# Third tile's stored pairs weighted and added by GpSimd in place of two diagonals on TensorE, in a two-layer retention and expert trunk

## The reference, cut to what matters

```
for l in range(2):
    h = modulate(rmsnorm(x, norm1_g[l]), sh1, sc1)
    x = x + g1 * mixer(h, ...)                 # retention and pooling branches
    h = modulate(rmsnorm(x, norm2_g[l]), sh2, sc2)
    x = x + g2 * moe(h, ...)                   # 16 experts, two for each token
return rmsnorm(x, final_g)

moe: expert_idx, weights = route(h)            # two experts of one group of four
     y[token] = sum over j in (0, 1) of weights[token, j] * expert(expert_idx[token, j], h[token])
```

## Time and profile before

| | |
|---|---|
| median of three runs | 1477.68 us (1476.87 to 1478.13) |
| the profiled execution, its own time | 1476.83 us |
| its span, first to last instruction | 1475.2 us |
| TensorE busy | 1441.6 us (98%) |
| VectorE busy | 1133.5 us (77%) |
| ScalarE busy | 773.2 us (52%) |
| GpSimd busy | 147.6 us (10%) |
| mean granted clock of TensorE | 0.999 of full |

### The profile page before, as it was taken

One profiled execution on the slowest core, in us unless ns is written; L12 is line 12 of the kernel. 1 busy time (PEld: TensorE's weight loads), 2 busy tenths in 40 slices (PEclk: granted clock), 3 DMA queues, 4 the chain that ended last, 5 costly groups with the idle time before them and its releaser, 6 DMA issues.

```text
span 1475.2 us, 18824 instructions
## 1 busy us (share of the span) xinstructions
PE 1441.6 (98%) x6829; PEld 1154.6 (78%) x6829; DVE 1133.5 (77%) x1532; ACT 773.2 (52%) x1102; POOL 147.6 (10%) x139
## 2 busy tenths in 40 slices
PE   7999999999999999999989999999999999999997
PEld 2788877778877778888858888878888787888884
DVE  5774686555669999999977557854345899999998
ACT  4333433222346888888733344242233488888883
POOL 0000001000002211111100000100000122211110
PEclk9999999999999999999999999999999999999999
DMA  9855556455557999999956543642244879999995
GB/s 352 310 185 189 171 199 208 143 177 172 186 213 256 388 387 388 385 387 381 352 221 204 193 132 115 201 142 88 84 171 152 290 279 391 398 387 392 381 379 206
DMA packets 107413, 377.49 MB, mean 256 GB/s; under 512 B 16521, under 2 KB 16713, under 8 KB 106548
## 3 DMA queue, kind: packets, MB, share of 16 engines
q1 hardware_dynamic: 90864, 331.39, 61.6%
q0 software_dynamic: 15200, 40.62, 7.7%
q10 hardware_dynamic: 1252, 4.22, 0.8%
HBM read 361.32 MB, written 34.64 MB: 268 GB/s over the span
## 4 chain that ended last, share of the span: by engine, by line
PE 83%; DVE 12%; DMA 2%; ACT 1%; issue 1%; DVEq 1%; SPq 0%; ACTq 0%
PE ps L1758 25%; PE ps L1760 25%; PE ps L1759 24%; DVE w_lo L1509 3%; DVE w_lo_more L1509 3%; DMA raw<-w 2%; PE ps L1843 2%; PE ps L2017 1%; PE ps L1912 1%; PE ps L2066 1%; PE ps L1916 1%; DVE xgT_lo L1498 1%; DVE y_out L1532 1%; DVE w_lo L1006 1%; PE ps L1947 0%
## 5 line engine op out<-in xcount | busy, mean ns | idle before, releaser
L1006 DVE TENSOR_TENSOR w_lo<-raw,w_hi 128x1024 fp32r<-128x1024 f32 x132 | 161.4, 1224 | 213.2 <-ACT w_hi L650 211.9
L650 ACT ACTIVATE w_hi<-raw 128x1024 fp32r<-128x1024 f32 x132 | 139.1, 1058 | 333.5 <-PE ps L1760 332.5
L1509 DVE TENSOR_TENSOR w_lo<-raw,w_hi 128x1024 fp32r<-128x1024 f32 x188 | 224.6, 1221 | 3.8 <-ACT w_hi L835 3.0
L1758 PE MATMUL ps<-w_hi,hT_lo 128*128 128x512 f32 x512 | 206.2, 403 | 3.8 <-DVE hT_lo L1109 3.1
L1509 DVE TENSOR_TENSOR w_lo_more<-raw,w_hi_more 128x1024 fp32r<-128x1024 f32 x172 | 205.6, 1221 | 2.1 <-ACT w_hi_more L835 1.1
L835 ACT ACTIVATE w_hi<-raw 128x1024 fp32r<-128x1024 f32 x188 | 193.3, 1057 | 22.0 <-DMA raw<-w 12.7
L1760 PE MATMUL ps<-w_hi,hT_hi 128*128 128x512 f32 x512 | 200.0, 391 | 0.0
L1759 PE MATMUL ps<-w_lo,hT_hi 128*128 128x512 f32 x512 | 199.6, 390 | 0.0
L835 ACT ACTIVATE w_hi_more<-raw 128x1024 fp32r<-128x1024 f32 x172 | 176.7, 1057 | 25.2 <-DMA raw<-w 17.1
L1758 PE MATMUL ps<-hT_hi,w_lo 128*128 128x512 f32 x320 | 130.5, 408 | 0.0
L1760 PE MATMUL ps<-hT_hi,w_hi 128*128 128x512 f32 x320 | 124.9, 390 | 0.0
(11 more groups left out here) (285 smaller groups left out, 2632.7 us busy)
## 6 DMA issues: line engine op xcount, KB each, us to landing
raw<-w SPq DMA_DIRECT2D x590, 512.0 KB
h_rows<-h POOLq DMA_DIRECT2D x8, 1024.0 KB, 5.2
ahead<-w SPq DMA_DIRECT2D x4, 2048.0 KB, 11.8
x_state<-x POOLq DMA_DIRECT2D x2, 2048.0 KB, 9.9
y_rows<-x_in ACTq DMA_DIRECT2D x4, 1024.0 KB, 12.0
x<-x_state POOLq DMA_DIRECT2D x4, 1024.0 KB, 7.7
pair_early<-y_rows SPq DMA_DIRECT2D x4, 1024.0 KB, 6.3
x<-x_in SPq DMA_DIRECT2D x4, 512.0 KB, 14.1
```

Of the source, the lines that this page charges most:

```text
L650: act.activation(w_hi[:, q % W_SLOTS], stream_piece(l, q, r), ACT.Copy).then_inc(w_hi_ready, 1)
L1006: v.tensor_tensor(w_lo[:, q % W_SLOTS], stream_piece(l, q, r), w_hi[:, q % W_SLOTS], ALU.subtract).then_inc(raw_used, 1)
L1509: v.tensor_tensor(ring_lo(e * EXP + n), expert_piece(e, n), ring_hi(e * EXP + n), ALU.subtract).then_inc(raw_used, 1)
L1758: pe.matmul(dst, a_lo, b_hi, start=start, stop=False)
```

## The change

VectorE no longer writes `diag_w`, and TensorE no longer runs the four matmuls of f32 on it in each layer. GpSimd gets four instructions in each layer in their place, behind its work for expert 15: it multiplies `pair_2[:, 0]` by its column of weights in place, adds the product to x[:, 2], and does the same with `pair_2[:, 1]`. It waits for `hot_last_ready` and for the load of `pair_2` first, and raises `pairs_added` at the end. VectorE's `last_add` of tile 2 waits for `pairs_added`. Between the layers, `last_rows(l - 1, 2)` now stands before `norm_transposes(l, 0)` on TensorE.

```diff
-                for j in range(2):
-                    one = v.tensor_scalar(diag_w[:, j], ident, w_early[:, 4 * j + 2:4 * j + 3], None, ALU.mult)
                 one.then_inc(hot_last_ready, 1)
@@ last_add
                 v.wait_ge(last_added, l * NT + (t + 1))
+                if t == 2:
+                    v.wait_ge(pairs_added, l + 1)
@@ last_rows (TensorE)
-                                    start=t != 2, stop=True)
+                                    start=True, stop=True)
-            def last_rows_pairs(l):
-                pe.wait_ge(pair_in[2], (l + 1) * PAIR_DMAS[2])
-                pair_matmuls(0)
-                pair_matmuls(1)
@@ TensorE, start of layer 1
-                    last_rows_pairs(l - 1)
+                    last_rows(l - 1, 2)
                     norm_transposes(l, 0)
-                    last_rows(l - 1, 2)
@@ TensorE, end of layer 1
-                    last_rows_pairs(l)
                     last_rows(l, 2)
@@ GpSimd, behind the loop over the experts, in each layer
                     expert(l, e)
+                pool.wait_ge(hot_last_ready, l + 1)
+                pool.wait_ge(pair_in[2], (l + 1) * PAIR_DMAS[2])
+                for j in range(2):
+                    pool.tensor_scalar(pair_2[:, j], pair_2[:, j], w_early[:, 4 * j + 2:4 * j + 3], None, ALU.mult)
+                    pool.drain()
+                    one = pool.tensor_tensor(x[:, 2], x[:, 2], pair_2[:, j], ALU.add)
+                    if j == 0:
+                        pool.drain()
+                one.then_inc(pairs_added, 1)
                 with pool.If(count > 0):
```

More of the change, by code:

```diff
@@ L279, in build @@
         h_nat = sb("h_nat", [P, 2, D], F32, Dr)
-        diag_w = sb("diag_w", [P, 2, P], F32, Dr + 8192)
         h2 = [sb(f"h2_{t}", [P, D], F32, o) for t, o in enumerate((Dr, Dr + 4096, A, A + 4096))]
@@ L419, in build @@
         x_final = sem("x_final")
+        pairs_added = sem("pairs_added")
         ada_mac = sem("ada_mac")
```

## The result

The changed kernel takes 1496.39 us (median of four runs, 1494.40 to 1499.08), the kernel before 1477.91 us in the same comparison (four runs, 1476.87 to 1478.61). The ratio is 1.0128, with a 95% interval of 1.0116 to 1.0140: slower by 18.9 us (17.1 to 20.7). The profiled execution took 1496.41 us, its span is 1494.8 us, 19.6 us more than before. Forecast were 1488.2 us, and 1496 us as the end of the range.

A forecast was written before the change was run, and what follows sets the result against it. The prediction took VectorE to bound the kernel after layer 1 and to be what TensorE waits for between the layers. 6.9 + 1.3 + 2.3 = 10.5 us on 1476.83 us, plus 0.85 us for a median, gave 1488.2 us; range 1482 to 1496 us.

The forecast's parts named there:

- the stop on VectorE: After layer 1: VectorE's first normed output waits for final_g, queued behind GpSimd's arithmetic; 6.9 us, passed whole to the end.
- contention in the tail: After layer 1: GpSimd and VectorE block each other on SBUF, delaying GpSimd and the load; 1.3 us, bounds 0 to 2.6.
- contention between the layers: Between the layers: the two engines on SBUF delay VectorE's hT_lo and so TensorE; 2.3 us, bounds 0 to 4.7.
- So the removed work buys nothing: Both stages: TensorE's diagonals and VectorE's writing of diag_w lie under cover; worth 0, at most 3.4 us at each place.
- worth 0: Between the layers: the diagonals fill the hole before the turned tile 0, so removing them gains 0 us.
- the rival of full exclusion: Tail and between layers: engines exclude each other in full, and TensorE's clock may fall; 16.2 us, 1493.9 us, chance 0.25.
- several us once: On GpSimd: a first elementwise use might cost several us once, hidden in layer 0 up to 753.71; not in the sum.
- never waited at: After layer 1: VectorE's last_add of tile 2 would not wait for GpSimd, being behind the 6.9 us stop.
- the late row: After layer 1: final_g's load into scale_row lands at 1468.5, while VectorE wants it at 1461.62; 6.9 us.
- The middle of the bounds: Tail and between layers: SBUF contention taken midway between none and whole-instruction blocking; 1.3 us and 2.3 us.
- the forecast's own case: Tail and between layers: late row plus middling contention; 10.5 us, 1488.2 us, chance 0.50.
- The other side: Tail: cheap late row, GpSimd at VectorE's 1.22 us, landing 2.6 us, no contention; 2.7 us, 1480.4 us, chance 0.04.

The follow-up runs named there:

- kernel with the row early: Changed kernel with the load of final_g issued ahead of GpSimd's four instructions of layer 1; 1488.34 us, ratio 1.0062.
- kernel without arithmetic: Changed kernel without GpSimd's four instructions and the waits for them, tile 2's two weighted pairs left out; 1480.17 us, ratio 1.0012.
- the clock given back: Changed kernel without GpSimd's four instructions and their waits, plus unread matmuls of ones in both TensorE holes between the layers; 1476.97 us, ratio 0.9998.
- both gaps taken away: Changed kernel with a one-column multiplication and addition on GpSimd ahead of the wait for pair_2, in each layer; 1491.97 us, ratio 1.0088.
- kernel with the work beside: Kernel before plus GpSimd's four instructions into an unread scratch tile, final_g loaded early, one-column instructions ahead; 1484.04 us, ratio 1.0043.
- the one with only the small addition: Changed kernel with only a one-column addition on GpSimd ahead of the wait, no one-column multiplication; 1492.41 us.
- kernel with both edits: Changed kernel with final_g loaded ahead of GpSimd's arithmetic and a one-column multiplication and addition ahead of the wait; 1487.00 us, ratio 1.0062.

## Why the prediction was right and wrong

The sign and the chain in the tail were right: TensorE's removed work bought nothing, and the load behind GpSimd's arithmetic set the end. The time was 8 us short, and 0.4 us beyond the range. Term by term:

| term | predicted us | measured us |
|---|---|---|
| GpSimd's start, behind `y_out` of expert 15 | 1.1 | -0.3 |
| four instructions on GpSimd | 7.2 | 10.4 |
| gap between the first two | none | 5.2 |
| drains between the others, and issue | 0.8 | 0.3 |
| landing of `final_g` | 4.5 | 4.0 |
| less the room from that start until VectorE wants the row | -5.6 | -6.9 |
| the stop on VectorE: the last five rows together | 6.9 | 12.95 |
| contention in the tail | 1.3 | 0 |
| contention between the layers | 2.3 | 2.7 |
| wait at `last_add` of tile 2 between the layers | none | 3.3 |
| less TensorE's room between tile 2's `last_add` and tile 3's own rows | none | -1.5 |
| second fall of the clock | none | 1.7 |
| elsewhere | none | 0.5 |
| sum, against the span before | 10.5 | 19.6 |

The room is that of the kernel before: `last_add` of tile 2 ended at 754.93, and TensorE came to tile 3's own rows at 756.45. The kernel with the row early bears the split out: without the second fall it loses 4.5 us there, which is 2.7 + 3.3 - 1.5. The first fall of the clock, 1.9 us, lies beside VectorE's lateness and has no row of its own: without it TensorE would only have waited longer for `last_add` of tile 2. It shows by itself in the kernel without arithmetic, 1.8 us by the medians (0.3 to 3.1) and 2.4 us in the profile.

*The removed work.* "So the removed work buys nothing" held: with the clock given back the ratio is 0.9998. What I missed is that it cost something to remove it. I took work that fills a wait to be worth 0. I did compare a hole with the one at the end of the trace, but only in the rival of full exclusion, and for one hole of 6.4 us. A hole of 2.35 us and the small transposes behind it were enough, and so was the later one of 2.46 us. That step, "worth 0" for the diagonals between the layers, failed by 1.8 us (the kernel without arithmetic).

*The size of an instruction.* This is one of the two terms that made the forecast short. I bounded it between 1.22 and 2.66 us and took 1.8. The addition takes 2.34 us, the multiplication 2.85 us, above the upper bound. The reason given for going under the middle, that two of the four have one tile as input, was backwards: the one-input form is the slow one here. 3.2 us. By the estimate from the Trainium skill's page GPSIMD Engine Reference, section 3.1, the addition would take 2.25 us and the multiplication 0.9 us: the trace agrees on the addition and not on the multiplication, which is three times that.

*The gap.* The other. I named it under what would make the prediction wrong, as a first use of "several us once", and wrote that it would be hidden in layer 0. It came in each layer, so that the one in layer 1 lies on the path (5.2 us), and in layer 0 it was not hidden either: GpSimd was done at 759.8, 6 us after VectorE wanted its result. That `last_add` of tile 2 is "never waited at" was true only after layer 1, and there because the late row had stopped VectorE for longer: with the row early it waits 5.30 us. With both gaps taken away the loss fell to 13.0 us, and this does not give back the whole of them, since the additions then meet VectorE. The Trainium skill's page GPSIMD Engine Reference, section 2.1, says that the first call to a freshly loaded kernel pays about 6 us with no instruction in the profile. The gaps of 5.2 to 8.7 us are of that size and as invisible, but no run here shows that code is loaded in them, and they come again in layer 1.

*Contention.* The middle of the bounds was the wrong choice in kind, and its size came near by luck. Both engines exclude each other for whole instructions, but only in some pairs (below). The forecast had the loss before tile 0's `hT_lo`, which TensorE's first product waits for. That product starts at 750.19, not late at all beyond the offset of 0.2 us; what lost 2.7 us are the two `h_nat` instructions of tile 1, at 751.42 and 754.65. In the tail nothing was lost, because the additions began at 1469.18, when VectorE already stood still. Where the row is early it costs 1.7 us there (one VectorE instruction of 2.97 us), and 3.5 us with the one-column instructions in the kernel with the work beside.

*The start, the issue and the landing* were put 1.4, 0.5 and 0.5 us too late or too long: `pair_2` landed in 8.7 us, not 9.7, and with the queues idle the row took 4.0 us. They hid a part of the miss.

So the forecast's own case had the right chain in the tail with two terms short, by 3.2 and 5.2 us. The stage between the layers lost 6.2 us, near the 6.7 us of the rival with full exclusion and the clock, but by another path: no late first product, a wait at `last_add` instead, and holes of 2.2 to 2.5 us in place of one of 6.4. The other side lost on each of its conditions.

## What to carry to other kernels

Before work is moved to GpSimd, list what stands behind it in its queue: here one DMA issue, which nobody thinks of as part of the change, was a third of the loss by the profiles and half by the medians. Work that an engine does in time in which it would wait is not always free to remove: if it is TensorE, look at what keeps its granted clock up in that stretch, and price the products behind the hole at both levels. Where the trace has no row of the operation to be added, the range must reach past the longest instruction found, and take in a start-up in each stretch in which the engine did only DMA work before.

## What the runs showed of the hardware

- GpSimd at 128x1024 f32: an addition of two tiles takes 2.34 us, a multiplication by a column of scalars 2.85 us; VectorE's take 1.22 to 1.28 us.
- After a stretch of DMA issues the second elementwise instruction on GpSimd starts 5.2 to 8.7 us late, be it an addition behind a multiplication or the reverse, on one column as on 1024. Two of the same kind were not tried. It came in both layers of every kernel with the arithmetic, except the one with only the small addition, where a wait would cover it. One issue of a load between the small and the large instructions did not bring it back (0.24 us before the large addition at 1464.23 in the kernel with both edits).
- An addition on GpSimd and a VectorE instruction with two SBUF tiles exclude each other from start to end, in both directions (VectorE 1.23 us, up to 3.27 where it came second; GpSimd 2.34 us, up to 3.40 where it came second). VectorE's `last_add`, which reads PSUM and x, stayed at 1.22 us. The Trainium skill, page SBUF — State Buffer, section Who interferes with whom, says this, and the runs agree for the addition. For the multiplication they don't agree in full. It waits for a VectorE instruction that came first (3.62 us in place of 2.85), but VectorE instructions that start 0.46 to 0.71 us after one (742.12 in the changed kernel, 1459.65 in the kernel with the work beside) take 1.49 to 1.72 us, all ending as if released some 0.9 us after its start, and later ones take 1.28 us while it still runs. It seems to keep VectorE out for its first 0.9 us only; that was read from these rows and not tried by itself.
- In the changed kernel TensorE's granted clock fell to 0.50 at about 747.5 us, behind a hole of 2.35 us and in the eight small transposes that follow it, and again at about 761.1, at the end of a hole of 2.46 us. In the kernel with the row early it fell at about 748.9, in the second of two holes of 2.36 and 2.37 us, and stayed at 1.00 through the later hole of 1.76 us, so that the 1.7 us behind the second fall are not lost there. In the kernel without arithmetic the clock fell as well, and with matmuls of ones in the same holes it stayed at 1.00.
